# Recurrent mixer: pair products, masks and the values' shares computed in the solve stage, and one product of 128 columns with each solved triangle

## The reference

```python
def step(state, inp):
    r_t, w_t, k_t, v_t, kk_t, a_t = inp
    sa = jnp.einsum('bhvk,bhk->bhv', state, -kk_t)
    state = (state * w_t[:, :, None, :]
             + sa[..., None] * (kk_t * a_t)[:, :, None, :]
             + v_t[..., None] * k_t[:, :, None, :])
    y_t = jnp.einsum('bhvk,bhk->bhv', state, r_t)
    return state, y_t
```

## Time and profile before

| | us |
|---|---|
| median of 3 runs | 3984.0 |
| profiled execution, whole | 3991.45 |
| its span, first to last instruction | 3989.6 |
| PE busy | 3129.5 (78%) |
| DVE busy | 2525.9 (63%) |
| ACT busy | 1243.3 (31%) |
| POOL busy | 392.0 (10%) |

### The profile page before, as it was taken

One profiled execution on the slowest core, in us unless ns is written; L12 is line 12 of the kernel. 1 busy time (PEld: TensorE's weight loads), 2 busy tenths in 40 slices (PEclk: granted clock), 3 DMA queues, 4 the chain that ended last, 5 costly groups with the idle time before them and its releaser, 6 DMA issues. The chain is left out here.

```text
span 3989.6 us, 43287 instructions
## 1 busy us (share of the span) xinstructions
PE 3129.5 (78%) x15237; PEld 2490.5 (62%) x15237; DVE 2525.9 (63%) x4649; ACT 1243.3 (31%) x2047; POOL 392.0 (10%) x351
## 2 busy tenths in 40 slices
PE   5958984997628839977833982577999999999996
PEld 2945673664616736643312552567999899888885
DVE  1446553654368646554774236567999685788897
ACT  2223322543326325421120100133434343333332
POOL 0000000021002000210000110020001111122220
PEclk8975585998769859988956775888999999999998
DMA  4641124894202248945101000123496979999995
GB/s 176 242 144 43 43 96 178 347 361 166 104 19 80 101 172 348 360 165 201 63 9 27 1 1 6 69 80 116 149 306 213 336 233 351 364 364 391 391 383 205
DMA packets 232949, 738.15 MB, mean 185 GB/s; under 512 B 30742, under 2 KB 130454, under 8 KB 197414
## 3 DMA queue, kind: packets, MB, share of 16 engines
q1 hardware_dynamic: 204236, 514.30, 36.2%
q0 software_dynamic: 28512, 221.26, 14.9%
HBM read 660.48 MB, written 75.01 MB: 184 GB/s over the span
## 5 line engine op out<-in xcount | busy, mean ns | idle before, releaser
L2402 DVE TENSOR_TENSOR peer_mix_w_lo<-hT,peer_mix_w_hi 128x1024 fp32r<-128x1024 f32 x256 | 312.8, 1222 | 146.3 <-ACT peer_mix_w_hi L2335 145.3
L362 PE MATMUL peer_mix_risen<-peer_h_hi,peer_mix_w_hi 128*128 128x384 f32 x1024 | 353.1, 345 | 34.6 <-DVE peer_mix_w_lo L2402 34.4
L363 PE MATMUL peer_mix_risen<-peer_h_lo,peer_mix_w_hi 128*128 128x384 f32 x1024 | 346.4, 338 | 0.0
L364 PE MATMUL peer_mix_risen<-peer_h_hi,peer_mix_w_lo 128*128 128x384 f32 x1024 | 345.9, 338 | 0.0
L2335 ACT CAST peer_mix_w_hi<-hT 128x1024 fp32r<-128x1024 f32 x256 | 268.7, 1050 | 203.4 <-DMA hT<-in_peer_u 195.3
L1243 DVE TENSOR_TENSOR moe_blocks_gu_lo<-moe_raw,moe_blocks_gu_hi 128x2048 fp32r<-128x2048 f32 x112 | 251.5, 2287 | 56.9 <-ACT moe_blocks_gu_hi L1207 56.9
L2273 POOL DMA_INDIRECT peer_mix_got<-in_peer_uv,peer_mix_where x128 | 170.0, 1328 | 1038.2 <-DVE peer_sum_rows L2438 867.2
L362 PEld LDWEIGHTS peer_mix_risen<-peer_h_hi,peer_mix_w_hi 128*128 128x128 f32 x1024 | 195.6, 191 | 40.4 <-DVE peer_mix_w_lo L2402 40.2
L1207 ACT CAST moe_blocks_gu_hi<-moe_raw 128x2048 fp32r<-128x2048 f32 x112 | 207.6, 1906 | 30.9 <-PEq L68 22.5
L362 PE MATMUL peer_mix_low<-peer_mix_w_hi,peer_h_hi 128*128 128x512 f32 x516 | 203.2, 394 | 11.3 <-DVE peer_h_lo L2426 6.2
L363 PE MATMUL peer_mix_low<-peer_mix_w_lo,peer_h_hi 128*128 128x512 f32 x516 | 202.0, 391 | 0.0
(11 more groups left out here) (673 smaller groups left out, 7389.4 us busy)
## 6 DMA issues: line engine op xcount, KB each, us to landing
moe_raw<-in_moe_gate_up SPq DMA_DIRECT2D x32, 2048.0 KB
hT<-in_peer_u SPq DMA_DIRECT2D x128, 512.0 KB
hT<-in_peer_v SPq DMA_DIRECT2D x128, 512.0 KB
fox_o<-in_side_w SPq DMA_DIRECT2D x48, 512.0 KB, 4.3
peer_z<-peer_mix_z_out_rows SPq DMA_DIRECT2D x128, 192.0 KB
peer_mix_stage<-peer_w SPq DMA_DIRECT2D x128, 192.0 KB
peer_mix_stage<-peer_z SPq DMA_DIRECT2D x128, 192.0 KB
peer_w<-peer_mix_stage SPq DMA_DIRECT2D x36, 512.0 KB
```

What stands on the lines that cost most here:

```text
L362: nc.tensor.matmul(out, l_hi, r_hi, start=start, stop=False)
L363: nc.tensor.matmul(out, l_hi, r_lo, start=False, stop=False)
L364: return nc.tensor.matmul(out, l_lo, r_hi, start=False, stop=stop)
L2402: v.tensor_tensor(w_lo[:, i % 3], raw[raw_of(i)], w_hi[:, i % 3].bitcast(F32), ALU.subtract).then_inc(w_split, 1)
```

## The change

The alpha rows and the value's share lie side by side in a new tile `pairs` (for each head 64 columns of alpha, then 64 of the value's product), so that one product with the solved triangle gives both. For that the copies in `turn_cols` write through a view of three dimensions, and the turns come in the order beta, kappa, value, alpha.

The three pair products, now with kappa by rho second and beta by rho third, move into the solve stage, behind the products of the triangles on PE's queue. DVE masks the first two into `early` (two buffers) and the third into `later`, which holds all units: 8 units before the substitution, one after each of its steps 1 to 24. PE multiplies the value with both early matrices, and kappa's rows with the value spread over the spans, which POOL makes. ACT copies the three results to `pairs`, to `y` and to the buffers of the new states. The triangles are masked into `solved` itself, and POOL clears it once they have been stored, between two of its products. Both loads (masks and span) are waited for at the start.

In the span stage PE has per unit one product of 128 columns, two for the outputs and two for the states; the products run one unit ahead of the rest. DVE adds the output's second part and the states' second part to what is there, and multiplies the new states by the decays at the end, once per chunk. POOL spreads beta alone. Its masks aren't loaded any more, and two of its buffers lie in `o.kappa`.

```diff
     with Stage(nc, f"{name}_solve") as s:
...
             @block.gpsimd
             def _(pool):
-                nc.gpsimd.memset(solved[:], 0.0).then_inc(zeroed, 1)
+                pool.wait_ge(loaded, 32)
+                here = span[:].unsqueeze(2).to_broadcast([P, BLOCKS, RW_DIM])
+                for m, (t, c, h) in enumerate(units):
+                    if m >= 2:
+                        pool.wait_ge(mixed, m - 1)
+                    nc.gpsimd.tensor_tensor(value_in[:, m % 2], rows["value"][:, t, cols[m]].unsqueeze(1).to_broadcast([P, BLOCKS, RW_DIM]),
+                                            here, ALU.mult).then_inc(spanned, 1)
+                    if m == WAITING:
+                        pool.wait_ge(stored, 16 * BLOCKS)
+                        nc.gpsimd.memset(solved[:], 0.0).then_inc(zeroed, 1)
             @block.tensor
             def _(pe):
+                def open_(m):
+                    t, c, h = units[m]
+                    if m >= 2:
+                        pe.wait_ge(early_masked, m - 1)
+                        pe.wait_ge(later_masked, m - 1)
+                    for j, (left, right) in enumerate(((o.kappa, o.alpha), (o.kappa, o.rho), (o.beta, o.rho))):
+                        last = nc.tensor.matmul(pair[:, m % 2, j * P:(j + 1) * P], left[feats[m], c, toks[m]],
+                                                right[feats[m], c, toks[m]], start=True, stop=True)
+                    last.then_inc(tripled, 1)
+
+                def mix(m):
+                    t, c, h = units[m]
+                    value = rows["value"][:, t, cols[m]]
+                    pe.wait_ge(early_masked, m + 1)
+                    pe.wait_ge(spanned, m + 1)
+                    if m >= 2:
+                        pe.wait_ge(kept, 3 * (m - 1))
+                    nc.tensor.matmul(mid[:, m % 2, :RW_DIM], early[:, m % 2, 0], value, start=True, stop=True)
+                    nc.tensor.matmul(mid[:, m % 2, RW_DIM:2 * RW_DIM], early[:, m % 2, 1], value, start=True, stop=True)
+                    nc.tensor.matmul(mid[feats[m], m % 2, HALF:], rows["kappa"][:, t, cols[m]], value_in[:, m % 2],
+                                     start=True, stop=True).then_inc(mixed, 1)
...
+                open_(0)
+                for m in range(UNITS):
+                    if m + 1 < UNITS:
+                        open_(m + 1)
+                    mix(m)
+
+            @block.scalar
+            def _(act):
+                for m, (t, c, h) in enumerate(units):
+                    act.wait_ge(mixed, m + 1)
+                    nc.scalar.copy(pairs[:, t, heads[m], 1], mid[:, m % 2, :RW_DIM]).then_inc(kept, 1)
+                    nc.scalar.copy(y[:, t, CONV + cols[m].start:CONV + cols[m].stop], mid[:, m % 2, RW_DIM:2 * RW_DIM]).then_inc(kept, 1)
+                    nc.scalar.copy(new[c][feats[m], spans_of[m]], mid[feats[m], m % 2, HALF:].rearrange("p (n v) -> p n v", n=BLOCKS)).then_inc(kept, 1)
             @block.vector
             def _(dve):
                 v = nc.vector
-                dve.wait_ge(loaded, 16)
+
+                def mask(m):
+                    dve.wait_ge(tripled, m + 1)
+                    if m >= 2:
+                        dve.wait_ge(mixed, m - 1)
+                    v.tensor_tensor(early[:, m % 2], pair[:, m % 2, :2 * P].rearrange("p (j n) -> p j n", j=2), masks[:, 1:3],
+                                    ALU.mult).then_inc(early_masked, 1)
+                    v.tensor_tensor(later[:, m], pair[:, m % 2, 2 * P:3 * P], masks[:, 3], ALU.mult).then_inc(later_masked, 1)
+
+                dve.wait_ge(loaded, 32)
...
+                for m in range(WAITING):
+                    mask(m)
                 dve.wait_ge(spread, 16)
                 for i in range(1, SPAN):
...
                     v.tensor_reduce(t_cols[:, :i, i], prod[:, :i, :i], AX, ALU.add).then_inc(found, 1)
+                    if WAITING + i - 1 < UNITS:
+                        mask(WAITING + i - 1)
...
     with Stage(nc, f"{name}_spans") as s:
...
-                def open_(m):
+                def solve(m):
                     t, c, h = units[m]
                     if m >= 2:
...
                         pe.wait_ge(pq_kept, m - 1)
...
+                    both = pairs[:, t, heads[m]].rearrange("p a v -> p (a v)")
+                    nc.tensor.matmul(mid[:, m % 2, :P], solved[:, m], both, start=True, stop=True).then_inc(pq_done, 1)
...
+                    nc.tensor.matmul(out[feats[m], m % 2, :P], pq[:, m % 2, 0], later[:, m], start=True, stop=True)
+                    nc.tensor.matmul(out[:, m % 2, P:P + RW_DIM], later[:, m], pq[:, m % 2, 1], start=True, stop=True).then_inc(out_done, 1)
+                    pe.wait_ge(spread, m + 1)
                     pe.wait_ge(q_spread, m + 1)
...
                     nc.tensor.matmul(state[feats[m], m % 2, 0], pq[:, m % 2, 0], beta_in[:, m % 2], start=True, stop=True)
...
+                    nc.tensor.matmul(state[feats[m], m % 2, 1], rows["beta"][:, t, cols[m]], q_in[:, m % 2],
+                                     start=True, stop=True).then_inc(state_done, 1)
+
+                solve(0)
                 for m in range(UNITS):
                     if m + 1 < UNITS:
...
+                        solve(m + 1)
                     close(m)
...
+                dve.wait_ge(loaded, 16)
+                spread_q(0)
+                for m, (t, c, h) in enumerate(units):
+                    if m + 1 < UNITS:
+                        spread_q(m + 1)
+                    row = y[:, t, CONV + cols[m].start:CONV + cols[m].stop]
                     dve.wait_ge(out_done, m + 1)
                     v.tensor_tensor(lead[feats[m], c, toks[m]], out[feats[m], m % 2, :P], o.rho[feats[m], c, toks[m]],
                                     ALU.add).then_inc(out_kept, 1)
+                    v.tensor_tensor(row, row, out[:, m % 2, P:P + RW_DIM], ALU.add).then_inc(row_kept, 1)
                     dve.wait_ge(state_done, m + 1)
...
+                dve.wait_ge(new_kept, UNITS)
+                for c in range(RC):
+                    ends = o.grown[:, c, SPAN - 1::SPAN]
+                    v.tensor_tensor(new[c], new[c], ends.unsqueeze(2).to_broadcast([P, SPANS, RW_DIM]), ALU.mult).then_inc(ended, 1)
```

More of the change, by code:

```diff
@@ L1646, in rwkv @@
     own = ExitStack()
-    rows = {x: own.enter_context(nc.sbuf_tensor(f"{name}_{x}_rows", [P, TILES, RW], F32)) for x in ("alpha", "beta", "kappa", "value")}
+    rows = {x: own.enter_context(nc.sbuf_tensor(f"{name}_{x}_rows", [P, TILES, RW], F32)) for x in ("beta", "kappa", "value")}
+    pairs = own.enter_context(nc.sbuf_tensor(f"{name}_pairs", [P, TILES, RW_HEADS, 2, RW_DIM], F32))
+    rows_of = {x: [buf[:, t].rearrange("p (h v) -> p h v", v=RW_DIM) for t in range(TILES)] for x, buf in rows.items()}
@@ L1648, in rwkv @@
+    rows_of["alpha"] = [pairs[:, t, :, 0] for t in range(TILES)]
+    heads = [2 * c + h for _, c, h in units]
     cols_of = {"alpha": o.alpha, "beta": o.beta, "kappa": o.kappa, "value": o.value}
-    for x, buf in rows.items():
-        turn_cols(nc, g, f"{name}_turn_{x}", cols_of[x], RC, [buf[:, t] for t in range(TILES)])
+    for x, kept_rows in rows_of.items():
+        turn_cols(nc, g, f"{name}_turn_{x}", cols_of[x], RC, kept_rows)
     solved = own.enter_context(nc.sbuf_tensor(f"{name}_solved", [P, UNITS, P], F32))
+    later = own.enter_context(nc.sbuf_tensor(f"{name}_later", [P, UNITS, P], F32))
@@ L1652, in rwkv @@
     inner = nc.dram_tensor(f"{name}_inner", [BLOCKS, UNITS, SPAN, SPAN], F32, kind="Internal").ap()
     outer = nc.dram_tensor(f"{name}_outer", [BLOCKS, UNITS, SPAN, SPAN], F32, kind="Internal").ap()
+    lead = g.hT[:, :RC]
+    pieces = [flat(g.hT[:, RC:])[:, :SPANS * RW_DIM], flat(g.hT[:, RC:])[:, SPANS * RW_DIM:], g.mod[:, 0], g.mod[:, 1]]
+    new = [x.rearrange("p (n v) -> p n v", n=SPANS) for x in pieces]
+    spans_of = [slice(t * BLOCKS, (t + 1) * BLOCKS) for t, _, _ in units]
     with Stage(nc, f"{name}_solve") as s:
-        masks = s.sb("masks", [P, 4, P])
@@ L1658, in rwkv @@
-        m_all = s.sb("m_all", [P, UNITS, P])
+        masks, span = s.sb("masks", [P, 4, P]), s.sb("span", [P, BLOCKS])
         m_rows, t_cols = s.sb("m_rows", [P, SPAN, SPAN]), s.sb("t_cols", [P, SPAN, SPAN])
         prod = flat(g.hT[:, :SPAN * SPAN // SEQ]).rearrange("p (s t) -> p s t", s=SPAN)
+        early, value_in = s.sb("early", [P, 2, 2, P]), s.sb("value_in", [P, 2, BLOCKS, RW_DIM])
         acc = s.ps("acc", [P, 4, RC, P])
+        pair, mid = s.ps("pair", [P, 2, BANK]), s.ps("mid", [P, 2, BANK])
@@ L1670, in _ @@
                     part = slice(b * SPAN, (b + 1) * SPAN)
-                    sp.dma_start(inner[b].rearrange("m t s -> t m s"), m_all[part, :, part]).then_inc(stored, 16)
+                    sp.dma_start(inner[b].rearrange("m t s -> t m s"), solved[part, :, part]).then_inc(stored, 16)
                 sp.wait_ge(stored, 16 * BLOCKS)
@@ L1799, in _ @@
             def _(act):
-                for m, (t, c, h) in enumerate(units):
```

(6 more changed lines are left out.)

99 lines of the change are left out of this document (30 added, 69 removed).

## The result

The runs of the changed kernel took 3843.98, 3859.91, 3909.71 and 3924.06 us (median 3884.81), those of the kernel before beside them 3978.24 to 3989.3 (median 3985.12). The profiled execution took 3843.98 us, its span 3841.8; 3991.45 and 3989.6 before.

The account below looks back on a forecast made before the run. PE's instruction stream was taken to bound the span stage. Solve stage +38.7 and span stage -145.6 make -106.9 us; 3991.45 less that and 7.45 (profiled execution over median) gives 3877 us, range 3855 to 3928.

Parts of the forecast that it names:

- Which clock: Solve and span loops: PE assumed at 2.4 GHz in both, 1.99 and 2.15 us per unit; chosen, not read.
- Rival (1): PE stays at 1.2 GHz in the solve loop: +49 us, 3926 us, 15%; span stage instead 8%, both 4%.
- My first reason: For 2.4 GHz: in the solve stage PE was at 1.00 with the same kind of 64-row products back to back.
- My second reason: For 2.4 GHz: the old unit's PE waits for ACT's two copies, 0.35 us for the second, are absent from the new loops.
- The rule on the clock: TensorE's clock: slow is the default, sustained activity releases it; the prediction said the trace agrees. No size given.
- The sums by stage: Solve stage +38.7 us, ending some 88 us after its start; span stage 81.7 us against 227.3, so -145.6.
- The wait for the second load: Solve stage's start: DVE waits for masks and span, 5.2 us against 2.6, so +2.6 us.
- Rival (2): Solve stage: PE's stream isn't the bound and the moved work hides fully; 3858 us, 7%.
- Rival (3): Solve stage: DVE's substitution products and POOL block each other over SBUF, 24 waits, 14.7 us; 3892 us, 5%.
- (4): Solve and span loops run in lock-step at 1.2 GHz without overlap: +188 us, 4065 us, slower than before, 3%.
- (5): The change only shifts work: the solve stage grows by what the span stage loses; 3984 us, 3%.

Follow-up runs that it names:

- start_after: Changed kernel plus two bursts of 12 unread products on PE, ahead of the first masks' wait and of the first mix: median 3814.73 us, ratio 0.9732.
- fox_before: Kernel before the change plus 24 unread TensorE products in the first attention stage: median 3910.67 us.
- best: Changed kernel plus 24 unread products in the first attention stage and two bursts of 12 in the solve stage: median 3804.15 us, ratio 0.9749.
- after_again: Changed kernel run again with nothing edited: 3850.45, 3856.5, 3927.17 and 3932.56 us.
- fox_after: Changed kernel plus 24 unread TensorE products in the first attention stage: median 3861.33 us.
- loop_after: Changed kernel plus one unread product in every unit of the solve loop: median 3824.3 us, ratio 0.9759.
- filled_before: Kernel before, with 24 unread products in the first attention stage and two per unit in the old span loop: median 3861.28 us.
- two_products: Changed kernel with attention and solve-stage bursts, its 128-column product split into two of 64: median 3859.78 us, ratio 0.9815.
- two_held: Changed kernel with attention and solve-stage bursts, 128-column product split in two, 16 unread products at the span stage's head: median 3813.92 us.

## Why the prediction was right and wrong

- **The step that failed** is "Which clock": "the step that I chose and did not read is 2.4 GHz in both loops". It held for the span loop and not for the solve loop. Rival (1), +49 us for 1.2 GHz in the solve loop, is what happened (+46.8: 85.5 against the forecast 38.7, at 3.67 us per unit against its 3.62), and its 3926 us is where the changed kernel's slower group lies (3909.71 to 3932.56). My first reason for 2.4 GHz was that products of the same kind had run at 1.00. The first half of the triangles' products did so again; then PE stood still for 1.08 us for DVE, the clock fell at 2040.0 during the second half, and the loop ran at 1.2 GHz to its end. My second reason, that the new loops have no wait like that for ACT's copies, was right of the loop and no help: PE had records in 103.56 of 104 us at 0.50. start_after shows that work for PE around its two early waits keeps the clock; that the wait of 1.08 us is what took it is not shown by itself.
- **The rule on the clock.** The prediction has from the Trainium skill ("TensorE: Matmul & The Clock Gate"; it stands in "Part 1: The HAM clock gate", not in the section that the prediction names) that the slow clock is the default and sustained activity releases it, and says that the trace agrees. It agrees with the first half: the clock was 0.50 from 281 to 314 us, where PE had nothing. It does not agree with the second: from 400 to 500 us PE had records all the time, and the clock was 0.50. The measurement decides; the trace of before had this row, and a kernel in which that stage gets its clock was a case to price.
- **The term that was missing** is the first attention stage, 144.7 or 215.9 us in either kernel. All three runs given of before were of its slower kind and nothing in their times hinted at a second; its clock of 0.50 under a full PE was in the trace, and I did not ask what it would do if it rose. This -71 us, and no step of the change, put the compared time below the range. That 3852 lies only 25 us from the forecast 3877 is luck: the misses of +46.8 and -71.2 us point opposite ways. With the attention stage alike in both, the change gives 49 to 65 us where the forecast had 107.
- **The sums by stage** held where the clock was the assumed one: solve stage 87.6 at 2.4 GHz (88), its loop 2.02 (1.99), span stage 77.1 (81.7), unit 2.16 (2.15). The whole, with both loops at 2.4 GHz, is fox_before to best: -106.5 us against -106.9. The 4.6 us of the span stage are its start: in these profiles the clock rose 5.9 to 6.1 us after the stage's first product, sooner than the forecast had it. That is not so every time: 13.5 us in after_again, 21.3 in fox_after (stage 83.9 us) and 29.3 in loop_after (87.4).
- **The wait for the second load** was put at 5.2 us after the old pair of loads; it took 3.1, against 2.6 before.
- **Rival (2)** (full hiding) is out: PE's unit never went under 2.0 us. **Rival (3)** exists as a mechanism, but costs nothing in this kernel's solve stage (no overlap) and under 0.5 us in its span stage. **Rivals (4) and (5)**: the solve loop had the 1.2 GHz of (4), but not the lock-step (3.67 us per unit, not 5.15; DVE's mask overlaps PE's mix, 2088.42 beside 2088.31), and the sum isn't zero.
- **What the change itself is worth** when both kernels have the clock: filled_before to best, -57.1 us; by stages +35.4 (solve) and -91.8 (spans). The old loop pays there for 64 unread products, and the two are from different sets of runs, so the change itself is worth at most about this.

Not settled: what took the clock in the solve stage, why the attention stage comes up at one clock or the other when nothing in the program differs, why the clock fell again there in one run with the burst, and why the same span loop gets its clock after 6 us in one execution and 29 in another.

## What to carry to other kernels

Before costing a change of a TensorE loop, price its stage at both clocks, and do the same for every stage whose row shows a full PE at 0.50: such a stage is a term of the sum, and of the spread of the runs. Where a loop stays at 1.2 GHz behind a short wait of PE, a dozen unread products at that wait are a cheap thing to try, ahead of any rearrangement (here they took 47 us off the solve stage). An edit can change a stage by ten times the time of the products that it adds or splits (62 us against 5 in two_products, and 55 us less for 64 products more in filled_before), so test it with the clock held.

## What the runs showed of the hardware

- A busy PE isn't enough for the full clock: the solve loop had PE records in 103.56 of 104 us at 0.50, the first attention stage in all of 50 us at 0.50. The same solve loop, begun at 2.4 GHz, stays there (0.98). It isn't so of every stage: in two_held the attention stage, at 1.00 for 82 us, fell to 0.50 at 408.4.
- One stage of the same code took 144.7 and 144.9 us (after, after_again) or 215.9 and 210.6 (before, start_after), and the times of either unedited kernel fall in two groups as far apart. With 24 unread products it took 146.2 and 146.6, and all 14 runs of fox_before and fox_after are of the faster group.
- VectorE's product with two SBUF inputs beside GpSimd's: 1.00 instead of 0.76 us at 576 elements, 0.48 instead of 0.20 at 36; GpSimd's own 0.756 instead of 0.611 in the mean; a sum with one input is unchanged.
